# Regrouping TensorE's small products in the RWKV-7 scan of a two-block transformer kernel

## What is computed

```python
def _wkv7_scan(r, w, k, v, a, b):
    def step(S, inp):
        r_t, w_t, k_t, v_t, a_t, b_t = inp
        sa = jnp.einsum('bhvk,bhk->bhv', S, a_t)
        S = S * w_t[:, :, None, :] + sa[..., None] * b_t[:, :, None, :] + v_t[..., None] * k_t[:, :, None, :]
        return S, jnp.einsum('bhvk,bhk->bhv', S, r_t)
...
    y = _wkv7_scan(rh, dh, kh, vh, -kk, kk * ah)
    mu = jnp.mean(y, axis=-1, keepdims=True)
    var = jnp.mean(jnp.square(y - mu), axis=-1, keepdims=True)
    y = (y - mu) * lax.rsqrt(var + GN_EPS)
...
    y = y + jnp.sum(rh * kh * r_k.astype(F32), axis=-1, keepdims=True) * vh
```

## Time and profile before

| what | value |
|---|---|
| median of 3 runs | 2839.78 us (2837.72 to 2839.84) |
| profiled execution | 2839.95 us, of which the span 2837.9 us |
| TensorE busy | 2808.0 us (99%) |
| VectorE busy | 1723.7 us (61%) |
| ScalarE busy | 1219.7 us (43%) |
| DMA | 489.19 MB, mean 172 GB/s |

### The profile page before, as it was taken

One profiled execution on the slowest core, in us unless ns is written; L12 is line 12 of the kernel. 1 busy time (PEld: TensorE's weight loads), 2 busy tenths in 40 slices (PEclk: granted clock), 3 DMA queues, 4 the chain that ended last, 5 costly groups with the idle time before them and its releaser, 6 DMA issues.

```text
span 2837.9 us, 49890 instructions
## 1 busy us (share of the span) xinstructions
PE 2808.0 (99%) x20837; PEld 2481.8 (87%) x20837; DVE 1723.7 (61%) x2527; ACT 1219.7 (43%) x1824; POOL 90.4 (3%) x167
## 2 busy tenths in 40 slices
PE   9999999999999999999999999999999999999999
PEld 8999878888888888899788888999998888888887
DVE  6467747666566544654667665766566566665444
ACT  5355544333334334643544444564453333334443
POOL 1000000000000000000000000000003100000000
PEclk9999999999999999999999999999999999999999
DMA  7566455555555555555444435545556655555554
GB/s 248 192 168 179 152 178 164 192 178 188 189 184 192 184 187 192 170 176 165 117 111 119 109 98 163 135 121 192 187 177 208 227 181 192 178 187 192 184 190 148
DMA packets 372639, 489.19 MB, mean 172 GB/s; under 512 B 13399, under 2 KB 182694, under 8 KB 372214
## 3 DMA queue, kind: packets, MB, share of 16 engines
q1 hardware_dynamic: 362752, 471.49, 52.5%
q0 software_dynamic: 6432, 12.08, 1.5%
q10 hardware_dynamic: 3302, 3.39, 0.4%
HBM read 477.79 MB, written 9.11 MB: 172 GB/s over the span
## 4 chain that ended last, share of the span: by engine, by line
PE 90%; DVE 7%; ACT 2%; issue 1%; DMA 1%; DVEq 0%; SPq 0%; ACTq 0%
PE psum L354 20%; PE psum L356 10%; PE psum L358 6%; PE psum L360 6%; PE psum L359 6%; PE psum L566 6%; PE psum L570 5%; PE psum L568 5%; PE psum L695 4%; PE psum L697 4%; PE psum L696 4%; PE psum L755 3%; PE psum L758 3%; PE psum L757 3%; DVE w_lo L344 3%
## 5 line engine op out<-in xcount | busy, mean ns | idle before, releaser
L344 DVE TENSOR_TENSOR w_lo<-w_raw,w_hi 128x1024 fp32r<-128x1024 f32 x728 | 859.4, 1221 | 797.0 <-ACT w_hi L335 797.0
L335 ACT ACTIVATE w_hi<-w_raw 128x1024 fp32r<-128x1024 f32 x728 | 732.2, 1052 | 1161.7 <-PE psum L356 592.1
L354 PE MATMUL psum<-act,w_hi 128*128 128x512 f32 x2816 | 988.4, 394 | 4.9 <-DVE w_lo L344 1.8
L356 PE MATMUL psum<-act,w_lo 128*128 128x256 f32 x2816 | 789.9, 280 | 0.0
L354 PEld LDWEIGHTS psum<-act,w_hi 128*128 128x128 f32 x2816 | 528.8, 188 | 132.1 <-DVE w_lo L344 11.1
L356 PEld LDWEIGHTS psum<-act,w_lo 128*128 128x128 f32 x2816 | 529.4, 188 | 0.1
L358 PE MATMUL psum<-act,w_hi 128*128 128x256 f32 (+3 forms) x1360 | 386.7, 284 | 2.1 <-DVE w_lo L344 1.0
L360 PE MATMUL psum<-act,w_lo 128*128 128x256 f32 (+3 forms) x1360 | 386.0, 284 | 0.0
L359 PE MATMUL psum<-act,w_hi 128*128 128x256 f32 (+3 forms) x1360 | 385.8, 284 | 0.0
L566 PE MATMUL psum<-act,w_hi 128*128 128x256 f32 (+1 forms) x1280 | 385.6, 301 | 0.0
L570 PE MATMUL psum<-act,w_lo 128*128 128x256 f32 (+1 forms) x1280 | 361.4, 282 | 0.0
(11 more groups left out here) (397 smaller groups left out, 2792.2 us busy)
## 6 DMA issues: line engine op xcount, KB each, us to landing
w_raw<-w_in SPq DMA_DIRECT2D x128, 1024.0 KB, 5.7
w_raw<-w_down SPq DMA_DIRECT2D x88, 1024.0 KB, 5.1
w_raw<-w_gate_up SPq DMA_DIRECT2D x88, 1024.0 KB, 5.1
w_raw<-w_gate SPq DMA_DIRECT2D x44, 1024.0 KB, 5.2
w_raw<-w_up SPq DMA_DIRECT2D x44, 1024.0 KB, 5.2
w_raw<-w_out SPq DMA_DIRECT2D x16, 1024.0 KB, 5.1
w_raw<-w_o SPq DMA_DIRECT2D x16, 1024.0 KB, 5.0
w_raw<-w_branch_a SPq DMA_DIRECT2D x8, 1024.0 KB, 5.0
```

What stands on the lines that cost most here:

```text
L335: nc.scalar.activation(w_hi[:, s % 2, 2 * h:2 * h + 2, 0:wd], w_raw[:, s % RAW, 2 * h:2 * h + 2, 0:wd], ACT.Copy).then_inc(hi_ready, 1)
L344: nc.vector.tensor_tensor(w_lo[:, s % 2, 2 * h:2 * h + 2, 0:wd], w_raw[:, s % RAW, 2 * h:2 * h + 2, 0:wd], w_hi[:, s % 2, 2 * h:2 * h + 2, ...
L354: pe.matmul(dst.rearrange("p (h n) -> p h n", h=2), w1, both_parts, start=first, stop=False, skip_group_check=True)
L356: return pe.matmul(dst[:, 0:n], w0, act_hi[:, k, tok], start=False, stop=last, skip_group_check=True)
```

## The change

TensorE: each pair opens with one `side(8)`. Behind it stand together the centring of the pair before, the bonus, the turns and the blocks' products, and then one `side(11)`. The blocks' products wait for `ah`, no longer for `bv` and ScalarE's `toks`; TensorE waits for ScalarE's `toks` ahead of the first 32x32 products instead. The `side(2)` ahead of the centring is gone, `side(1)` stands only ahead of the last.

ScalarE: sides of 5 (pair 0: 2), 4, 6 and 1 become 1, 6, 0 and 10, and the one at the pair's end 4 for 5 (8 in the last pair).

VectorE: the sides of 1, 2, 2, 2 and 6 slots in the pair's opening go, and one `side(13)` stands behind `i8t`. The centred copy comes behind `rh` instead of behind `rk`.

```diff
@@ rwkv_pe
+            def center(j):
+                pe.wait_ge(*rd.after(("ys", j)))
+                pe.matmul(psum[:, 3, 0:SEQ], T["head_center"], ys, start=True, stop=True) \
+                    .then_inc(*rp.did(("yc", j)))
+
             for j in range(8):
-                side(4)
+                side(8)
+                if j > 0:
+                    center(j - 1)
                 pe.wait_ge(*rd.after(("rk", j)))
...
-                side(3)
-
                 pe.wait_ge(*rd.after(("kh", j)))
...
                 mm.then_inc(*rp.did(("toks", j)))
-                side(3)
-
-                pe.wait_ge(*rd.after(("bv", j)))
-                pe.wait_ge(*ra.after(("toks", j)))
-
+                pe.wait_ge(*rd.after(("ah", j)))
...
-                side(7)
+                side(11)
...
                 dve("n8t")
+                act("toks")
                 product(4, n8t, n8, "p2")
...
-                side(2 if j < 7 else 1)
-                pe.wait_ge(*rd.after(("ys", j)))
-                pe.matmul(psum[:, 3, 0:SEQ], T["head_center"], ys, start=True, stop=True) \
-                    .then_inc(*rp.did(("yc", j)))
+            side(1)
+            center(7)
             side(8)
@@ rwkv_act
-                side(5 if j else 2)
+                side(1)
                 s.wait_ge(*rd.after(("run", j)))
...
-                side(4)
+                side(6)
                 s.wait_ge(*PEA("toks"))
...
                 ins.then_inc(*ra.did(("toks", j)))
-                side(6)
...
-                side(1)
+                side(10)
                 evac("p2", rd.after(("p2t", j)), p2, 4)
...
-                side(5 if j < 7 else 8)
+                side(4)
@@ rwkv_dve
-                side(1)
                 v.wait_ge(*ra.after(("a", j)))
...
-                if j > 0:
-                    centered(j - 1)
-                    side(2)
-                side(2)
                 v.wait_ge(*A_("kkn"))
                 v.tensor_tensor(bh, kkn, a_t, ALU.mult).then_inc(*D_("b"))
...
                 v.tensor_tensor(ar[:, 1], R_, ar[:, 1], ALU.mult).then_inc(*D_("rh"))
-                side(2)
+                if j > 0:
+                    centered(j - 1)
                 v.wait_ge(*rp.after(("toks", j)))
                 v.tensor_tensor(V_, psum[:, 0, 0:TOK], V_, ALU.mult).then_inc(*D_("bv"))
-                side(6)
...
                 TT(i8t, n8t, table_of("ident_blocks"), ALU.add).then_inc(*D_("i8t"))
+                side(13)
                 v.wait_ge(*PEA("p2"))
```

More of the change, by code:

```diff
@@ L1714, in transformer_pair_kernel @@
         for j in range(8):
-            rw_dve_steps += [(n, j) for n in ("a", "t1", "kf", "kkn", "rk")] + [("yc", j - 1)] * (j > 0)
-            rw_dve_steps += [(n, j) for n in ["b", "bh", "kh", "ah", "rh", "bv"] + INV_DVE
+            rw_dve_steps += [(n, j) for n in ("a", "t1", "kf", "kkn", "rk", "b", "bh", "kh", "ah", "rh")]
+            rw_dve_steps += [("yc", j - 1)] * (j > 0) + [(n, j) for n in ["bv"] + INV_DVE
                              + ["u1", "sd", "s1", "sh2", "x2", "u2"]]
```

## The result

The changed kernel takes 2853.46 us (median of 6 runs, 2852.15 to 2854.91), the kernel before 2840.57 (6 runs in the same comparison). The ratio is 1.0046 with a 95% interval of 1.0036 to 1.0057: slower, by some 13 us, where 3 us less were forecast and 2842 was the upper end of the range. The profiled execution took 2854.91 us with a span of 2852.8, 14.9 more than the span before.

What follows compares the result with a forecast made beforehand. The kernel was taken as bound by TensorE's own work. Terms of -5.1, -1.7, -1.6 and +5.6 summed to -2.8 us, forecast 2837.0 us; range 2830.5 to 2842, the forecast's own 2833.5 to 2841.

Steps and rivals of the forecast that it cites:

- late `ys`, `rk`, `kh`: TensorE's waits for these releases in the scan go, as eight slots now stand ahead of the small group: -5.1 us.
- slow stretch of pair 0: The 3.4 us at half clock in pair 0 go with the idle time ahead of them: -1.7 us.
- joints: One exit to and one entry from the side stream go between turns and blocks in each of 8 pairs: -1.6 us.
- waits for a bank: TensorE waits in five pairs until VectorE's gathered side(13) evacuates a side tile's bank: +5.6 us.
- Edits 1 and 2: Late releases of `ys`, `rk`, `kh` in the scan go, -5.1 us; pair 0's half-clock stretch goes, -1.7 us.
- Edit 3: Joints between turns and blocks on TensorE go: -1.6 us, bounds -2.5 and 0.
- full-size joints: Joints of centring and bonus with the side stream, taken at nothing; the -2.5 bound holds if they count.
- Edit 4: VectorE's sides gathered behind `i8t` make TensorE wait for banks in pairs 5, 6, 7, 0 and 1: +5.6 us.
- What else moves, at nothing: ScalarE's sides, VectorE's later steps, DMA queues and TensorE's two more slots in the scan cost nothing.
- Rival A: No wait for the banks in the scan, so 8.4 us are won: 2831.4 us; chance 0.24.
- Rival B: The new bank waits halve TensorE's clock, 1.7 us per stretch: 2840.4 to 2845.5 us; chance 0.13.
- Rival C: The wait moves into TensorE's small group, with `kh` or `ah` late behind the bonus: +2.4 us, 2839.4; chance 0.08.

Runs made afterwards that it cites:

- split_back: Changed kernel with VectorE's side(13) split into side(6) behind rh and side(7) behind i8t, and side(6) for side(8) behind the scan on VectorE and TensorE: 2830.68 us.
- counts_back: Changed kernel, but behind the scan VectorE and TensorE run side(6) for side(8): 2843.97 us.
- before_dve_ahead: Kernel before, but VectorE runs side(10) for side(8) behind the scan: 2852.68 us.
- evac_split: Changed kernel, but VectorE's side(13) is split into side(6) behind rh and side(7) behind i8t: 2840.63 us.
- dve_back: Changed kernel, but only VectorE runs side(6) for side(8) behind the scan: 2845.63 us.
- act_up: Changed kernel, but ScalarE runs side(6) for side(4) at the end of the last pair: 2852.01 us in one run.
- fetch_phase: Changed kernel with 64 more waits, for something long done, in TensorE's program ahead of the scan: 2855.66 us.

## Why the prediction was wrong, point by point
| term | forecast | in the traces |
|---|---|---|
| late `ys`, `rk`, `kh` | -5.1 | -5.1, none is left |
| slow stretch of pair 0 | -1.7 | -1.7 |
| joints | -1.6 | -2.7 (0.33 to 0.35 in each pair) |
| waits for a bank | +5.6 | +6.1 |
| waits without a releaser | 0 | +3.0 |
| `lft` and act, behind the scan | 0 | +4.9 |
| half clock behind these | 0 | +8.5 |
| DMA wait of L200 | 0 | +1.0 |

These sum to 14.0 of 14.9 us. The first row is counted as in the earlier trace rows, by the weight loader; counted so, the waits for a bank are 7.1 us.

**Edits 1 and 2** held. split_back carries them to the time.

**Edit 3** had the mechanism and missed the size. I took the joint between turns and blocks as one entry and one exit, 0.2 us. The two groups overlap besides, which I had not priced: 0.33 us went. The full-size joints gave nothing, as forecast (centring and bonus take 0.89 us together in pair 1 and as much apart), so that -2.7 lies beyond my lower bound of -2.5 for another reason than the one that bound stood for. By the rule of the Trainium skill (TensorEngine Tiling (Array Packing), "Key Properties") as I applied it, TensorE would have drained between them, for -0.8. No drain shows here: L1870 of 32 output rows starts among products of L1861 with 16. Whether these two count as different modes, which the rule asks for, no run here shows, so the trace speaks against my use of the rule and not against the rule.

**Edit 4** held to a tenth: 1.8, 1.7, 1.0, 0.9 and 0.2 us were forecast for pairs 5, 6, 7, 0 and 1; 1.88, 1.79, 1.08 and 1.00 were measured for the first four, and 0.3 is left of the 1.3 for the fifth. None stands in pairs 2 to 4. In pairs 6 and 7 the late evacuation is a gate tile's (L2820), not L1757. From start to start each costs some 0.15 us more than its idle time.

**"What else moves, at nothing"** is the step that failed, twice. It says that "TensorE's slots inside the scan rise from 248 to 250, taken from the next stage", and stops there. The count `21 + 31j` holds the same rise for VectorE, and I never asked what VectorE's next steps would meet. In the kernel before, all three engines leave the loop with 268 steps done. After the change two stand at 270 and ScalarE at 268. That cost 9.5 us by counts_back and 13.5 alone in before_dve_ahead. It is in no row of the scan; it is in the row of ScalarE's two squares, in the stage after it.

The second omission is SyncE's queue. I wrote "No DMA is moved on a queue", which is true of the instructions and not of their times: a weight load waits for VectorE's low parts, and thirteen steps in one block move the loads, and with them the instruction pieces, against TensorE's small products. evac_split shows the price: it took 12.8 us off, where the 6.1 us of bank waits and the 3.4 us of clock leave some 3 for these waits.

**Rival A**, 8.4 us won, is close to what the kernel does once both are mended: 2830.7 us against 2831.4. It was not a miscount, though; the waits were there. That the numbers are so close is in part luck: by the traces split_back's scan is 9.8 us shorter than before, 1.4 more than A's terms, while the medians differ by 8.5.

**Rival B** named the halved clock, but behind the bank waits. In the changed kernel's trace none of the five was followed by it. The rival isn't refuted, though: in four of the five other traces with the same waits (counts_back, dve_back, act_up, fetch_phase) the clock fell for 3.4 us right behind the 1.88 us of pair 5, and in fetch_phase behind the 1.80 of pair 6 too. In the changed kernel it fell behind a wait without a releaser (1.13 us, with 1.07 us busy in 2.20) and behind the two waits after the scan, 2.2 and 2.7 us. The Trainium skill (TensorE: Matmul & The Clock Gate, "What's actually happening") ties the fall to low activity before it; all three stretches agree.

**Rival C** did not occur: TensorE doesn't wait within the small group.

## What to carry to other kernels
Where programs on several engines walk one shared side stream by hand-written step counts, add up the counts of each engine at the end of the stage that is edited, and compare them with before. An offset that costs nothing inside the stage can be paid in the next one. And when side work is gathered into one block, list everything that its steps release: here banks for TensorE, and weight loads that shift the instruction loads.

## What was not expected of the hardware
- TensorE can stand idle for its own instructions: in all 26 waits without a releaser it goes on 2.2 to 2.8 us behind the first packet of a 16 KB piece, though the packet takes only 0.9 to 1.4 us. In the changed kernel's scan 55 to 242 products lie between the starts of two pieces.
- Products with 16 and 32 output rows overlapped, and the group was 0.33 us shorter than its parts with the side stream between them.
- The same wait of 1.88 us was followed by 3.4 us at half clock in four of six kernels and by none in two.
- Half-clock stretches of 3.4 us also stand in stages that no kernel here touches, not at the same places in every execution: at 421 us before, at 1172 in evac_split, at 300, 307 and 1174 in before_dve_ahead. A difference of 1.7 us between two traces can be that alone.
